# x turned by the host at the head of a two-block float32 kernel

## What is computed

```python
u = rms_norm(h, norm_mix_g[l])        # h is x: 256 x 1024
z = u @ w_in[l]                       # 1024 x 5640
qa, ka, va, qk_b, vb, ob, ib, fb, ga, gb = jnp.split(z, IN_SPLITS, axis=-1)
i_pre = (ib + b_igate[l]).transpose(0, 2, 1)
f_pre = (fb + b_fgate[l]).transpose(0, 2, 1)
```

## Time and profile before

| what | us |
|---|---|
| runs: median (lowest to highest) | 1342.9 (1342.3 to 1343.26) |
| the profiled execution, its own time | 1342.51 |
| its span, first to last instruction | 1340.7 |
| busy: TensorE, VectorE, ScalarE, GpSimd | 1335.0, 1070.0, 706.3, 135.4 |
| DMA: bytes moved, mean rate | 246.40 MB, 184 GB/s |

### The profile page before, as it was taken

The page is one execution under the profiler, slowest core; times in us unless marked ns, Lnnn a source line. Parts: engine busy times, 40 slices in busy tenths (PEclk is TensorE's granted clock), DMA queues, the critical chain, the costliest instruction groups (busy, mean ns, idle before and its releaser), DMA issues.

```text
span 1340.7 us, 17742 instructions
## 1 busy us (share of the span) xinstructions
PE 1335.0 (100%) x6445; PEld 1105.4 (82%) x6445; DVE 1070.0 (80%) x1882; ACT 706.3 (53%) x953; POOL 135.4 (10%) x158
## 2 busy tenths in 40 slices
PE   9999999999999999999999999999999999999999
PEld 8988888888888888887788888888888888888887
DVE  6995678778878877968678888888888788698777
ACT  6666446444464444577764444544445677644442
POOL 1352001020010000142010000100000432100000
PEclk9999999999999999999999999999999999999999
DMA  8744455675546555554346555465556442555562
GB/s 303 186 160 159 161 168 200 232 260 198 200 164 207 197 192 192 182 175 143 126 156 220 189 188 188 157 220 188 188 188 211 167 157 95 164 184 193 201 201 93
DMA packets 108817, 246.40 MB, mean 184 GB/s; under 512 B 5112, under 2 KB 9636, under 8 KB 108624
## 3 DMA queue, kind: packets, MB, share of 16 engines
q1 hardware_dynamic: 106576, 240.19, 52.7%
q0 software_dynamic: 1744, 4.70, 1.2%
q10 hardware_dynamic: 432, 0.66, 0.1%
HBM read 244.45 MB, written 1.07 MB: 183 GB/s over the span
## 4 chain that ended last, share of the span: by engine, by line
PE 97%; ACT 1%; DVE 1%; issue 0%; POOL 0%; DVEq 0%; ACTq 0%
PE ps L1765 27%; PE ps L1710 17%; PE ps L1712 16%; PE ps L1711 16%; PE ps L1770 14%; PE ps L1962 1%; PE ps L1736 1%; PE ps L2016 1%; PE ps L2000 1%; PE ps L2285 0%; DVE wlo L1568 0%; PE ps L2024 0%; PE ps L1927 0%; PE ps L2051 0%; PE ps L2057 0%
## 5 line engine op out<-in xcount | busy, mean ns | idle before, releaser
L1765 PE MATMUL ps<-whi,xx 128*128 128x512 f32 x1600 | 379.2, 389 | 0.0
L1765 PEld LDWEIGHTS ps<-whi,xx 128*128 128x128 f32 x1600 | 300.3, 188 | 62.3
L661 ACT ACTIVATE whi<-raw 128x2048 fp32r<-128x2048 f32 (+1 forms) x165 | 262.0, 1599 | 80.9 <-PE ps L1712 50.8
L1055 DVE TENSOR_TENSOR wlo<-raw,whi 128x2048 fp32r<-128x2048 f32 x105 | 239.9, 2288 | 49.1 <-ACT whi L661 48.3
L1257 DVE STREAM_TRANSPOSE sc<-sc 32x128 f32<-32x128 f32 x864 | 261.7, 303 | 12.9
L1060 DVE TENSOR_TENSOR wlo<-raw,whi 128x2048 fp32r<-128x2048 f32 x90 | 206.0, 2289 | 49.2 <-ACT whi L669 48.3
L669 ACT ACTIVATE whi<-raw 128x2048 fp32r<-128x2048 f32 x90 | 171.8, 1909 | 67.0 <-PE ps L1770 67.0
L1710 PE MATMUL ps<-whi,hhi 128*128 128x512 f32 (+1 forms) x506 | 198.2, 392 | 0.0
L1770 PE MATMUL ps<-wlo,xx 128*128 128x512 f32 x800 | 197.6, 389 | 0.0
L1712 PE MATMUL ps<-whi,hlo 128*128 128x512 f32 (+1 forms) x506 | 196.7, 389 | 0.0
L1711 PE MATMUL ps<-wlo,hhi 128*128 128x512 f32 (+1 forms) x506 | 196.5, 388 | 0.0
(11 more groups left out here) (293 smaller groups left out, 1196.7 us busy)
## 6 DMA issues: line engine op xcount, KB each, us to landing
raw<-in_ffn_gate_up SPq DMA_DIRECT2D x88, 1024.0 KB, 5.1
raw<-in_ffn_w_down SPq DMA_DIRECT2D x44, 1024.0 KB, 4.9
raw<-in_w_in SPq DMA_DIRECT2D x40, 1024.0 KB, 5.1
raw<-in_gate_up SPq DMA_DIRECT2D x22, 1024.0 KB, 5.1
raw<-in_w_out SPq DMA_DIRECT2D x12, 1024.0 KB, 4.9
raw<-in_w_down SPq DMA_DIRECT2D x11, 1024.0 KB, 5.0
raw<-in_w_mem_kv SPq DMA_DIRECT2D x4, 1024.0 KB, 5.2
raw<-in_w_proj_a SPq DMA_DIRECT2D x2, 1024.0 KB, 5.1
```

Of the source, the lines that this page charges most:

```text
L661: ins = act.activation(whi[:, slot, v], raw[:, slot, v], ACT.Copy)
L1055: dve.tensor_tensor(wlo[:, u % 3, v], raw[:, u % 3, v], whi[:, u % 3, v], ALU.subtract)\
L1765: pe.matmul(ps[:, banks[r], :], x(4 * half + k, P * r, P)[part], whi[:, slot, 512 * k:512 * k + 512], start=half == 0 and k == 0 and part ...
```

## The change

The host hands in x a second time, turned (`x_t`: partition, column chunk, row). It is loaded into `memT`, which is free at that time, in two pieces of one chunk (128 KB) and three of two chunks. QA's two units are loaded in eight pieces of 256 KB, each behind its x. TensorE no longer turns x; it multiplies chunk by chunk, with the low of a weight piece one chunk behind. `idle(9)` replaces `idle(8)` and `idle(6)`. VectorE casts the first two weight pieces. x itself (for the residual and the mean squares) is loaded behind KA's first unit, the bias loads behind that, and KA's second unit, now in halves like the first, behind those. The identity's load moves from the front of ScalarE's queue to chunk 3, the other constants' load to the end of chunk 7, which is behind x's last piece. The gate products move from behind unit 0 to behind unit 1, with the `cwr` transpose; the four tiny products move from behind unit 1 to behind unit 2, and VectorE's gate inputs from its unit 0 to its unit 1.

```diff
         @block.sync
...
-            for h in range(2):
-                for r in range(RT):
-                    v = slice(512 * h, 512 * h + 512)
-                    sp.dma_start(res[:, r, v], t["x"][0, r * P:(r + 1) * P, v]).then_inc(x_full[h], 16)
-                if h == 0:
-                    for k, s in enumerate((quarter_full, half_full[0])):
-                        sp.dma_start(raw[:, 0, 512 * k:512 * k + 512], w_in[P * k:P * k + P, 0:512]).then_inc(s, 16)
-                    half_unit(0, 1, raw_full[0])
+            def x_part(c, n):
+                sp.dma_start(xt[:, c:c + n, :], t["x_t"][:, c:c + n, :]).then_inc(xt_full[c], 16)
+
+            def w_part(u, k):
+                row = P * (4 * u + k)
+                sp.dma_start(raw[:, u, 512 * k:512 * k + 512], w_in[row:row + P, 0:512])\
+                    .then_inc(raw_full[u] if k == 3 else part_full[3 * u + k], 16)
+
+            def half_unit(u, h):
+                if u == 3:
+                    sp.wait_ge(lo_done, 1)
+                sp.dma_start(raw[:, u % 3, 1024 * h:1024 * h + 1024].rearrange("p (a b) -> p a b", a=2),
+                             cols(w_in, 4 * (u - KA) + 2 * h, 2, 512, 512))\
+                    .then_inc(raw_full[u % 3] if h else half_full[u - KA], 16)
+
+            for c in range(KC):
+                if c < 2:
+                    x_part(c, 1)
+                elif c % 2 == 0:
+                    x_part(c, 2)
+                w_part(c // 4, c % 4)
             sp.dma_start(wif[:, :, :], t["wif"]).then_inc(wif_full, 16)
-            half_unit(1, 0, half_full[1])
-            half_unit(1, 1, raw_full[1])
+            half_unit(KA, 0)
+            half_unit(KA, 1)
+            for r in range(RT):
+                sp.dma_start(res[:, r, :], t["x"][0, r * P:(r + 1) * P, :]).then_inc(x_full, 16)
             sp.dma_start(bif[:, 0:BH], across(t["b_igate"][0])).then_inc(bias_full, 16)
             sp.dma_start(bif[:, BH:2 * BH], across(t["b_fgate"][0])).then_inc(bias_full, 16)
             sp.dma_start(cwr[:, :], t["conv_w"][0].rearrange("j (c p) -> (j c) p", p=P)).then_inc(bias_full, 16)
-            wide(KA, w_in, 512)
+            half_unit(KA + 1, 0)
+            half_unit(KA + 1, 1)
...
         @block.gpsimd
...
+            pool.wait_ge(ident_full, 16)
             for r in range(RT):
                 pool.tensor_scalar(rdg0[:, r, :], ident, rstd[:, r:r + 1], None, ALU.mult).then_inc(diag0_ready, 1)
...
         @block.scalar
...
-            act.dma_start(cst[:, 0:P], t["consts"][:, 0:P]).then_inc(ident_full, 16)
             act.dma_start(gcol[:, :], t["gcol"]).then_inc(gcol_full, 16)
...
             act.wait_ge(gcol_full, 16)
...
+            for c in range(KC):
+                if c < 2 or c % 2 == 0:
+                    act.wait_ge(xt_full[c], 16)
+                if c == 3:
+                    act.dma_start(cst[:, 0:P], t["consts"][:, 0:P]).then_inc(ident_full, 16)
+                act.activation(xhi[:, c, :], xt[:, c, :], ACT.Copy, scale=gain_col(N_MIX, c)).then_inc(xhi_done, 1)
+                if c > 1:
+                    hi_part(c // 4, c % 4)
+            act.dma_start(cst[:, P:C_W], t["consts"][:, P:C_W]).then_inc(cst_full, 16)
             act.wait_ge(wif_full, 16)
             act.activation(wifs[:, :, 0:8], wif[:, :, :], ACT.Copy).then_inc(wif_hi, 1)
-            act.wait_ge(x_full[0], 16 * RT)
-            act.wait_ge(x_full[1], 16 * RT)
+            hi_half(KA, 0)
+            hi_half(KA, 1)
+            act.wait_ge(x_full, 16 * RT)
             act.activation(xn[:, 0, :], res[:, 0, :], ACT.Square, scale=DM ** -0.5, accum_out=ss[:, 0:1]).then_inc(sq_done, 2)
...
         @block.vector
...
+            for c in range(KC):
+                if c < 2:
+                    dve.wait_ge(part_full[c], 16)
+                    v = slice(512 * c, 512 * c + 512)
+                    dve.tensor_copy(whi[:, 0, v], raw[:, 0, v]).then_inc(quarter_hi, 1)
+                dve.wait_ge(xhi_done, c + 1)
+                dve.scalar_tensor_tensor(out=xlo[:, c, :], in0=xt[:, c, :],
+                                         scalar=gain_col(N_MIX, c), in1=xhi[:, c, :], op0=ALU.mult, op1=ALU.subtract)\
+                    .then_inc(xlo_done, 1)
+                lo_part(c // 4, c % 4)
...
         @block.tensor
...
-            idle(8)
+            idle(9)
+
+            def high(c):
+
+                u, k = c // 4, c % 4
+                if c < 2:
+                    pe.wait_ge(quarter_hi, c + 1)
+                elif k == 3:
+                    pe.wait_ge(hi_done, u + 1)
+                else:
+                    pe.wait_ge(part_hi, k + 2 if u else 1)
+                pe.wait_ge(xhi_done, c + 1)
+                for r in range(RT):
+                    pe.matmul(ps[:, r, :], x(c, P * r, P)[0], w(u, 512 * k, 512)[0], start=c == 0, stop=False)
...
-            pe.wait_ge(ident_full, 16)
-            turn_x(0)
-            idle(6)
+            for c in range(KC):
+                high(c)
+                if c > 0:
+                    w_low(c - 1)
+                x_low(c)
+            w_low(KC - 1)
...
-                if u == 0:
+                if u == 1:
...
                     pe.wait_ge(wif_lo, 1)
...
-                if u == 1:
                     pe.wait_ge(bias_full, 48)
+                    pe.wait_ge(ident_full, 16)
                     pe.transpose(ps[:, 5, 0:32], cwr[:, :], ident[0:32, 0:32]).then_inc(gate_ps, 1)
+                if u == 2:
                     pe.wait_ge(cst_full, 16)
                     pe.wait_ge(gate_copied, 2)
...
+    given["x_t"] = np.asarray(inputs["x"])[0].reshape(SEQ, KC, P).transpose(2, 1, 0)
```

More of the change, by code:

```diff
@@ L1301, in _, with lo_part @@
             dve.memset(pr[:, 0, 0:P], 0.0).then_inc(warm_ready, 1)
+            def lo_part(u, k):
+                if u == 0 and k < 2:
+                    dve.wait_ge(quarter_hi, k + 1)
+                elif k == 3:
+                    dve.wait_ge(hi_done, u + 1)
+                else:
+                    dve.wait_ge(part_hi, k + 2 if u else 1)
+                v = slice(512 * k, 512 * k + 512)
+                dve.tensor_tensor(wlo[:, u, v], raw[:, u, v], whi[:, u, v], ALU.subtract)\
+                    .then_inc(lo_done if k == 3 else part_lo, 1)
@@ new lines, in gate_inputs @@
+            def gate_inputs():
+                dve.wait_ge(rstd_ready, 2)
+                dve.wait_ge(bias_full, 48)
+                dve.wait_ge(gate_ps, 3)
+                for r in range(RT):
+                    ins = dve.scalar_tensor_tensor(out=gates[:, r, :], in0=ps[:, 4, 8 * r:8 * r + 8],
+                                                   scalar=rstd[:, r:r + 1], in1=bif[:, :], op0=ALU.mult, op1=ALU.add)
+                ins.then_inc(gate_dve, 1)
+                dve.wait_ge(gate_dve, 1)
+                dve.scalar_tensor_tensor(out=rh(0), in0=f_pre, scalar=-1.0, in1=f_pre, op0=ALU.mult, op1=ALU.max)\
+                    .then_inc(gate_dve, 1)
+                link(dve.tensor_scalar(rh(72), f_pre, 0.0, None, ALU.min))
@@ L1374, in _ @@
                                                  op0=ALU.mult, op1=ALU.subtract).then_inc(qk_lo_done, 1)
-                if u < 7 and u != 4:
+                if u == 0:
+                    gate_sums()
+                    lo_half(KA + 1, 0)
+                    lo_half(KA + 1, 1)
+                if u == 1:
+                    gate_inputs()
+                if 0 < u < 7 and u != 4:
                     lo(u + 3)
@@ L2026, in _ @@
             pe.wait_ge(warm_ready, 1)
-            idle(8)
-            def turn_x(half):
-                pe.wait_ge(x_full[half], 16 * RT)
-                for b in (2 * half, 2 * half + 1):
-                    for c in (2 * half + b, 2 * half + b + 2):
-                        bank, a = turn_at(T_MIX, c)
-                        for r in range(RT):
-                            ins = pe.transpose(ps[:, bank, a + P * r:a + P * r + P], res[:, r, P * c:P * c + P], ident)
-                    ins.then_inc(tr_ps, 1)
@@ new lines, in x_low, with w_low @@
+            def x_low(c):
+                pe.wait_ge(xlo_done, c + 1)
+                for r in range(RT):
+                    pe.matmul(ps[:, r, :], x(c, P * r, P)[1], w(c // 4, 512 * (c % 4), 512)[0], start=False, stop=False)
+            def w_low(c):
+                u, k = c // 4, c % 4
+                pe.wait_ge(lo_done if k == 3 else part_lo, u + 1 if k == 3 else 3 * u + k + 1)
+                for r in range(RT):
+                    ins = pe.matmul(ps[:, r, :], x(c, P * r, P)[0], w(u, 512 * k, 512)[1], start=False, stop=c == KC - 1)
+                if k == 3:
+                    ins.then_inc(unit_used, 1)
@@ new lines, in halved @@
+            def halved(u, banks):
+                for h in range(2):
+                    pe.wait_ge(lo_done if h else half_lo, u + 1 if h else u - KA + 1)
+                    for r in range(RT):
+                        for k in (2 * h, 2 * h + 1):
```

(5 more changed lines are left out.)

120 lines of the change are left out of this document (38 added, 82 removed).

## The result

| | before | after |
|---|---|---|
| runs: median (lowest to highest), us | 1342.9 (1342.3 to 1345.1) | 1345.08 (1344.3 to 1347.5) |
| the profiled execution, its span | 1342.51, 1340.7 | 1344.42, 1342.5 |
| ratio, 95% interval | | 1.0019 [1.0012, 1.0026] |

Slower by 2.2 us, where 1.8 us faster was predicted, and outside the range. (Ratios are formed over undisturbed executions, so they need not be the quotient of the medians.)

A forecast was written before the change was run, and what follows sets the result against it. TensorE, 97% of the chain, was taken to bound the kernel, so head time won is kept: 2.92 less 0.6 (pieces) and 0.5 (bias) gives 1.8 us, 1340.7 profiled, 1341.1 median; range 1339.8 to 1343.4.

The forecast's parts named there:

- VectorE behind the head: VectorE from 29.2 us: its start hangs on unit 4's unmoved load; TensorE has 2.3 us of room there, 2.7 at most.
- Start of the first product: Head: TensorE's first product of x with a weight starts at 4.95 instead of 7.00, 2.05 us won.
- Transposes: Head: TensorE no longer transposes x; the second eight win 0.87 us, the first eight are in the 2.05.
- the signs that it named for being wrong: First product after 5.5, holes after piece 3, products 0.45 apart, or a conv transpose that waits past 20.
- those for being right: First product near 4.95, two short holes before 8, conv transpose near 19.1, VectorE from 29.2 unmoved, no wait at 56-58.
- Supply of the pieces: Head: TensorE stalls 0.3 us at piece 1 and 0.3 at piece 2, together 0.6; later pieces arrive in time.
- The bias stall: Conv weights' transpose waits for the bias loads: TensorE there at 18.6, bias at 18.8 or 20.1; 0.5 us taken.
- 2.92: Upper limit of the gain in us: 2.05 from the earlier first product plus 0.87 from the transposes.
- The second: Rival: loads keep 341 GB/s up to the bias; stall 1.1 to 2.7, time 1341.7 to 1343.3; chance 0.17.
- The third, the clock: Rival: TensorE's clock rises late or falls back in QA, making it slower, 1345.5 to 1351; chance 0.07.
- The fourth: Rival: waits only change place, TensorE held 2 us or more at pieces 1 to 3; gain 0 to 0.8; chance 0.10.
- Edits costed at nothing: Moved steps (x's norm and copy, VectorE's gate inputs, waits, x's bytes twice) claimed covered by slack, costing 0.

The follow-up runs named there:

- e14: Changed kernel with GpSimd's seven small row-spreading loads made three loads of arrays the host laid out by partition; 1343.17 us, ratio 1.0002.
- e9: e12 with one row tile of QA rotated ahead of the gate inputs and the other behind unit 4's low; 1344.68 us, ratio 1.0013.
- e10: e9 with x's pieces issued on ScalarE's queue instead of between the weight pieces on SP's; 1343.73 us, ratio 1.0001.
- e11: e8 with the three loads of e14 in place of GpSimd's seven; 1341.27 us, ratio 0.9986.
- e2: Changed kernel with QA's evacuation ahead of ScalarE's high of unit 4 and its rotation ahead of VectorE's gate inputs; 1343.15 us, ratio 1.0000.
- e12: e2 with the conv weights' transpose and its bias wait also moved behind KA's first unit; 1343.35 us, ratio 1.0002.
- e126: e12 with x_t laid out so that each pair of pieces is contiguous; 1342.95 us, ratio 1.0002.
- e4: Changed kernel with dummy matmuls in the three holes of TensorE's head; 1345.25 us, ratio 1.0020.
- e8: e9 with x_t laid out so that each pair of pieces is contiguous; 1345.52 us, ratio 1.0018.
- e15: Kernel before the change with the three loads of e14 in place of GpSimd's seven; 1342.96 us, ratio 1.0000.

## Why the prediction was wrong

**The step that failed** is "VectorE behind the head". It said that VectorE's start at 29.25 hangs on unit 4's load "and that does not move", and that TensorE has 2.3 us of room. Both halves were wrong. The start moved by 1.8 us: the gate inputs wait for the tiny products behind KA's first unit, which the prediction put at about 25.3 and costed at nothing; they came at 27.5. Unit 4's load moved as well, from 24.4 to 25.7, behind the larger head. And the room was looked for where VectorE meets TensorE, at 56 to 58, not where the late work goes next: through the buffer that VectorE's low frees to the load of unit 9. There the room was 0.4 us, and at 110 us (the wait in the earlier trace rows, 0.2 us, already not zero) none. That row was read as a wait too short to matter; it also said that ScalarE arrives at that point no sooner than TensorE. Of the two halves it is the room that cost the time: in e14 VectorE starts even later (31.44) and nothing is lost behind the mark, and in e9 it starts at 26.5 and 3.0 us are lost there, because the load took 13.0 us.

**Start of the first product**: right (5.07 against 4.95). **Transposes**: right. Of the signs that it named for being wrong one came, a conv transpose that waited past 20; of those for being right, no wait at 56 to 58 came too, and did not mean that VectorE's lateness was harmless.

**Supply of the pieces** was mis-sized: 0.6 predicted. The distance between the starts of products tells what it was: 0.23 is usual, and at 5.40, 6.69, 7.03, 9.01 and 9.34 it was 0.34, 0.81, 0.34, 1.05 and 0.33, together 1.7 us more. The pace of the earlier trace rows from 4.6 to 7 (341 GB/s) was taken over; it was 216, so the second weight piece landed at 6.2 and piece 2's at 8.3.

**The bias stall** was mis-sized, within its bounds: 1.2 against 0.5. TensorE came at 19.75 instead of 18.6, and the last of the three loads was in at 20.9, later than either estimate (18.8, 20.1). That is the slow early pace again: 256 GB/s over the first 11 us are 2.8 MB where the prediction had 3.17, and 0.36 MB are 0.9 us at its 398 GB/s, which takes its later estimate (the constants ahead of the bias) to 21.0. So this stall and the one of the pieces go back to the same slow start of the loads. (The 2.2 us that the prediction put between the bytes and the bias took 383 GB/s past 11.0 us, where the earlier trace rows has 222; by that row they are 2.0.) The sum for the head is 2.92 less 0.12, 1.7 and 1.2, about -0.1; the mark at 45 us has -0.36, and the rest was not taken apart.

**Rivals.** The second had the stall's size (1.1 to 2.7, bias by 19.7 to 21.3) but not its reason: from 7 us on the loads ran at 398 GB/s, not at 341. The Trainium skill's limit of about 358 GB/s for one core (page "DMA: Bandwidth & Descriptors", section Specifications) was exceeded once more. The third, the clock, named the right side, but not what the median lost. A rise as late as it feared does come: in e10's profiled execution the first ten products are 0.43 us or more apart, up to 10.48, in e11's the first six are 0.41 or more apart, up to 7.18. Its argument against this, a rise by 4.84, was read from one execution. But in the changed kernel's own profiled execution the dummies are 0.11 apart from 4.05 on, ahead of any product, and it was late all the same. Falls go with the slowest executions: 4 of the changed kernel's 15 have a mean granted clock of 0.999 and took 1346.6 to 1347.5, and the other eleven, at 1.000, took 1344.3 to 1346.2, all of them more than the median before. The fourth came close for the head, whose stalls at the pieces were 1.7 us, and had nothing of the rest. No rival was a load far behind the head. **"Edits costed at nothing"** asked what covers each moved step, but not what a later VectorE would collide with on the DMA engines.

## What to carry to other kernels

When a step moves later, follow it past the next meeting with the bounding engine: which buffer it frees, which load that starts, what else is on the DMA engines by then, and how long before its use the load landed until now. Here a wait of 0.2 us on an engine that is 97% of the chain marked a dead heat, a place with no room. And if a win in one stage is not kept, split the span at a mark that every version has; here head and rest told in one line per run which side a loss was on.

## What was not expected of the hardware

- **Row-spreading loads.** Seven loads of 448 KB in all, beside a 1 MB load: 44 GB/s at a DMA share of 0.73, and 9.9 to 13.2 us for that load wherever the first of the seven was issued ahead of it; three loads of the same bytes laid out by partition: 237 GB/s and 5.8 us in e14, 6.4 to 6.5 us in the three other kernels with them. The Trainium skill, page "DMA: Bandwidth & Descriptors", section Specifications, asks for at least 512 B in a transfer for the full rate. Six of the seven had rows of 256 B, which fits; the seventh had 2 KB. The edit also ended the reading of one source row 128 times and made three loads of seven, so no run here tells size, source and number apart.
- **Who comes first.** In e2, e12 and e126 the same seven loads were there, but the first was issued 0.6 us behind the unit's load (42.9 against 42.3 in e2), not ahead of it (41.4 against 43.0 in the changed kernel), and the unit's load took 7.1 to 7.5 us. That points to the order of issue, and not to the earlier rotation as such, as the reason why e2 lost its wait at 112; e9 rotates as early (26.5 against 26.0) and kept it. No run changed the order of issue alone, so this is not shown.
- **The clock behind a wait.** After waits of 1.4 us (e12) and 2.3 us (e4) with TensorE idle, its products were 0.43 apart for some 3 us, granted clock 0.50, which is 1.2 GHz. In e8 the granted clock was 0.50 from 60.5 to 63.9 us, behind a wait of 1.6 us that ended at 59.1. After the same wait of 1.4 us in e126 it stayed at 1.00.
- **The clock's rise.** TensorE has the same order of work in the kernel before and in e15, dummies from 1.05 on and then eight transposes:

```profile
4.84 1.07 PE L2035 MATMUL ps<-cst,res 128*128 128x128 f32 x8
```

```profile
4.74 1.76 PE L2033 MATMUL ps<-cst,res 128*128 128x128 f32 x8
```

Before (the first line), the transposes are 0.11 us apart, the upper level of 2.4 GHz; in e15 they are 0.21 apart, the lower level, as the first dummies are in both, and 0.11 comes only with the second dummies, at 6.34. So the first product starts at 7.60 there, 0.6 us later. The Trainium skill, page "TensorE: Matmul & The Clock Gate", part 1, says of the rise that its point differs from run to run for one kernel; these two traces, with one order of work up to there, agree.
